# Two-block transformer kernel on one core: attention steps of block 2 in a new order, band copies on ScalarE's queue, memory projections in block 1

## What is computed

```python
z = jnp.einsum('bsd,df->bsf', x, w_in[l])
q_na, k_na, v_na, q_g, k_g, v_g, q_m, gate_logits = jnp.split(z, _split_points(), axis=-1)
y_na = ...   # neighbourhood attention, 8 heads of 64, keys of a 32-column band on an 8 x 64 grid
y_gqa = ...  # grouped-query attention, 8 query heads, 2 key heads of 64, norm and rotary first
mkv = jnp.einsum('bmd,df->bmf', mem, w_mem_kv[l])
mk, mv = jnp.split(mkv, 2, axis=-1)
y_mem = ...  # 4 heads of 128 over the 256 memory tokens
branches = jnp.stack([y_na, y_gqa, y_mem], axis=2)
proj = jnp.einsum('bsgk,gkd->bsgd', branches, w_branch[l])
gates = jax.nn.sigmoid(gate_logits + b_gate[l]).reshape(B, S, N_BRANCH, D)
merged = jnp.sum(gates * proj, axis=2)
mix = jnp.einsum('bsd,de->bse', merged, w_out[l])
x = layer_norm(DN_ALPHA * x + mix, ln1_g[l], ln1_b[l])
ffn = expert_choice_ffn(x, w_router[l], w_gate_up[l], w_down[l])   # 16 experts, 64 tokens each
x = layer_norm(DN_ALPHA * x + ffn, ln2_g[l], ln2_b[l])
```

## Time and profile before

| | us |
|---|---|
| median of 3 runs | 1814.62 |
| lowest, highest | 1810.46, 1818.32 |
| the profiled execution's own time | 1814.75 |
| its span, first to last instruction | 1812.8 |

### The profile page before, as it was taken

The page is one execution under the profiler, slowest core; times in us unless marked ns, Lnnn a source line. Parts: engine busy times, 40 slices in busy tenths (PEclk is TensorE's granted clock), DMA queues, the critical chain, the costliest instruction groups (busy, mean ns, idle before and its releaser), DMA issues.

```text
span 1812.8 us, 20763 instructions
## 1 busy us (share of the span) xinstructions
PE 1603.3 (88%) x7998; PEld 1136.4 (63%) x7998; DVE 745.2 (41%) x1091; ACT 516.2 (28%) x805; POOL 93.0 (5%) x144
## 2 busy tenths in 40 slices
PE   5989798999999989985799999998499999999994
PEld 4677677878878868864577787877333434434332
DVE  4454655334334344844434434355523222322235
ACT  4353424222221222243334433232021112111211
POOL 2000000000000001310111111000200000000000
PEclk9999579999999999987899999998599999999997
DMA  5222012323323335123112113337099999999993
GB/s 190 68 70 70 1 43 74 94 93 93 93 93 93 95 103 151 46 82 112 52 37 69 46 60 97 124 116 309 1 351 416 415 413 415 409 421 416 416 418 127
DMA packets 146038, 307.89 MB, mean 170 GB/s; under 512 B 8288, under 2 KB 99808, under 8 KB 129568
## 3 DMA queue, kind: packets, MB, share of 16 engines
q1 hardware_dynamic: 142592, 296.84, 44.5%
q0 software_dynamic: 2928, 9.02, 1.4%
q10 hardware_dynamic: 432, 0.81, 0.1%
HBM read 300.35 MB, written 4.56 MB: 168 GB/s over the span
## 4 chain that ended last, share of the span: by engine, by line
PE 73%; DMA 9%; DVE 8%; ACT 4%; issue 4%; SPq 1%; ACTq 0%; DVEq 0%
PE bank L948 11%; PE bank L1574 10%; PE bank L1575 9%; PE bank L1576 9%; DMA RING<-w_gu 5%; PE bank L1582 4%; PE bank L1583 4%; PE bank L1584 4%; DMA RING<-w_down 3%; PE bank L1621 2%; PE bank L923 2%; PE bank L1591 2%; PE bank L1592 2%; PE bank L1593 2%; PE bank L1709 2%
## 5 line engine op out<-in xcount | busy, mean ns | idle before, releaser
L1574 PE MATMUL bank<-XH,WH 128*128 128x512 f32 x768 | 305.6, 398 | 13.3 <-DVE WL L1278 12.2
L1575 PE MATMUL bank<-XL,WH 128*128 128x512 f32 x768 | 302.1, 393 | 0.0
L1576 PE MATMUL bank<-XH,WL 128*128 128x512 f32 x768 | 301.8, 393 | 0.0
L1278 DVE TENSOR_TENSOR WL<-RAW,WH 128x2048 fp32r<-128x2048 f32 (+1 forms) x91 | 194.2, 2134 | 178.9 <-ACT WH L1106 178.9
L948 PE MATMUL bank<-RING,XS 128*64 128x512 f32 x488 | 221.1, 600 | 16.9 <-DMA RING<-w_gu 9.0
L949 PE MATMUL bank<-RING,XS 128*64 128x512 f32 x496 | 224.7, 600 | 0.0
L1106 ACT ACTIVATE WH<-RAW 128x2048 fp32r<-128x2048 f32 (+1 forms) x91 | 161.8, 1778 | 170.8 <-PE bank L1584 124.8
L1574 PEld LDWEIGHTS bank<-XH,WH 128*128 128x128 f32 x768 | 146.6, 191 | 46.6 <-DVE WL L1278 13.5
L1576 PEld LDWEIGHTS bank<-XH,WL 128*128 128x128 f32 x768 | 146.0, 190 | 30.9
L1575 PEld LDWEIGHTS bank<-XL,WH 128*128 128x128 f32 x768 | 146.3, 190 | 30.3 <-issue 0.2
L948 PEld LDWEIGHTS bank<-RING,XS 128*64 128x64 f32 x488 | 63.4, 137 | 147.4 <-issue 142.6
(11 more groups left out here) (280 smaller groups left out, 2497.1 us busy)
## 6 DMA issues: line engine op xcount, KB each, us to landing
RING<-w_gu SPq DMA_DIRECT2D x123, 1024.0 KB, 13.7
RING<-w_down SPq DMA_DIRECT2D x64, 1024.0 KB, 11.7
RAW<-w_in SPq DMA_DIRECT2D x66, 512.0 KB, 4.8
RAW<-w_ffn_in SPq DMA_DIRECT2D x44, 512.0 KB, 4.6
RAW<-w_ffn_out SPq DMA_DIRECT2D x20, 512.0 KB, 4.3
RAW<-w_out SPq DMA_DIRECT2D x16, 512.0 KB, 4.7
RAW<-w_branch SPq DMA_DIRECT2D x24, 256.0 KB, 3.1
ONCE<-w_gu SPq DMA_DIRECT2D x5, 1024.0 KB, 11.1
```

The source lines that it names most:

```text
L1278: V.tensor_tensor(WL[:, u % 2, :n], RAW[:, u % 2, :n], WH[:, u % 2, :n].bitcast(F32), ALU.subtract).then_inc(s["w_lo"], 1)
L1574: T.matmul(bank[:, :st.nt], wh[:, k, c], hi, start=k == 0, stop=False)
L1575: T.matmul(bank[:, :st.nt], wh[:, k, c], lo, start=False, stop=False)
L1576: ins = T.matmul(bank[:, :st.nt], wl[:, k, c], hi, start=False, stop=k == st.K - 1)
```

## The change

**The lag.** In the three attentions of block 2, T, C and O of an iteration stand two iterations later instead of one, N one iteration later instead of none, and T and C stand ahead of X of the current iteration:

```diff
         turn = (((s_step, 0), (w_step, 0), (t_step, 1), (c_step, 1), (o_step, 2), (fill_step, 0)) if kind == "stick" else
-                ((s_step, 0), (x_step, 0), (t_step, 1), (c_step, 1), (n_step, 0), (fill_step, 0), (o_step, 1)))
+                ((s_step, 0), (t_step, 2), (c_step, 2), (x_step, 0), (n_step, 1), (fill_step, 0), (o_step, 2)))
```

```diff
     def na_band():
-        bands.append(add("band", dict(band=16 * 16), half=len(bands)))
+        bands.append(add("band", {f"band{len(bands) // 4}": 16 * 4}, half=len(bands) // 4, h=len(bands) % 4))
...
+            elif k == "band":
+                wait(act, "evA", st.at)
+                wait(act, "evD", st.at)
+                cols = slice(256 * st.half, 256 * st.half + 256)
+                bs = (0, 8, 24, 32)[st.h]
+                for b in range(2):
+                    for a in range(2):
+
+                        act.dma_start(VB[(2 * b + a) * 32:(2 * b + a) * 32 + 32, st.h, :, cols],
+                                      VN[a * 64 + bs:a * 64 + bs + 32, b::2, cols]).then_inc(s[f"band{st.half}"], 16)
```

```diff
-            9: [lambda: add("lsplit", dict(yhi=4, ylo=4), after=qkv[1])], 12: [lambda: out_half(0, 0)]}
+            9: [lambda: add("lsplit", dict(yhi=4, ylo=4), after=qkv[1])], 10: [memk(0)], 12: [memk(1)],
+            14: [lambda: out_half(0, 0)]}
...
     rms(X, XN, D, after=plan[-1])
+    memv(0)()
     tx(XN, XH, XL, KT, TT, scale=V_GFFN, feeds="x")
...
     fin = rms(X, X, D, grow=GFIN, after=plan[-1])

+    mem_last = memv(1)()
     save = add("save", dict(saved=16))
```

```diff
-    small = pieces_of(nak(1), nav(1), memk(0), memk(1)) + [memv(0), memv(1)] + pieces_of(gate(0, 0))
-    slots = (0, 1, 2, 3, 4, 5, 6, 7, 8, 10, 12, 14)
+    small = pieces_of(nav(1), nak(1), *(gate(0, j) for j in range(4)))
+    slots = (0, 1, 2, 3, 5, 6, 8, 9, 11, 12, 14, 15)
     fill = {i: [f] for i, f in zip(slots, small)}
-    fill[3].append(na_band)
-    na_last = attention("na", 4, 4, fill, lambda i: bands[i // 8])
+    for i in range(1, 5):
+        fill.setdefault(i, []).append(na_band)
+    na_last = attention("na", 4, 4, fill, lambda i: bands[4 * (i // 8) + 3])
...
-    small = pieces_of(gqm(1), branch(0, 0), *(f(0, j) for j in range(1, 4) for f in (gate, branch)))
+    small = pieces_of(gqm(1), *(branch(0, j) for j in range(4)), gate(1, 0), gate(1, 1))
...
-    small = pieces_of(*(f(1, j) for j in range(4) for f in (gate, branch)))
+    small = pieces_of(branch(1, 0), branch(1, 1), gate(1, 2), branch(1, 2), gate(1, 3), branch(1, 3), gate(2, 0),
+                      gate(2, 1))
...
-    add("reload", {})
-    for j in range(4):
-        whole(gate(2, j))
-        whole(branch(2, j))
+    for f, j in ((branch, 0), (branch, 1), (gate, 2), (branch, 2), (gate, 3), (branch, 3)):
+        whole(f(2, j))
+        if f is branch and j == 0:
+            add("reload", {})
```

More of the change, by code:

```diff
@@ L142, in build @@
     QM = at("QM", R0 + 32, [P, 4, S])
-    RT = at("RT", 181.5, [P, 3, 640])
+    RT = at("RT", R0 + 48, [P, 3, 640])
     GFIN = at("GFIN", R0 + 16, [P, D])
     LNR = at("LNR", 64, [P, 2, D])
-    GT = at("GT", 76, [P, 2, S])
+    GT = at("GT", 72, [P, 2, 2, S])
     MG = at("MG", R0 + 48, [P, KT, S])
@@ L203, in build @@
                lexp lgl lt lm2 lsq lin lrec ysq yn yhi ylo qk mx e_ab msk p tr ptA ptD pv o rope rxn rope_p
-               ms_hi ms_lo saved band x2h x2l xal lgp lgs afp af top ixp icc rcp pn ohi""".split()
+               ms_hi ms_lo saved band0 band1 x2h x2l xal lgp lgs afp af top ixp icc rcp pn ohi""".split()
     names.extend(["rms_q", "rsd_q"])
@@ L347, in build, with memk, memv @@
     win, win2 = w_in[0], w_in2[0]
+    def memk(j):
+        return lambda: unit(w_memkv[0], UC * j, KT, "F", "copy", dst=lambda r: MKT[:, 2 * j + r, :], src="m", nt=M)
+    def memv(j):
+        return lambda: unit(w_memkv[0], 512 + UC * j, KT, "T", "copy", dst=lambda r: MV[:, :, UC * j:UC * j + UC],
+                            src="m", nt=M)
     rms(X, XN, D, ready=x_in)
@@ L418, in gqm, with gate_home @@
         return (win2, 2304 + UC * j, KT, "F", "scaled"), dict(dst=lambda r: QM[:, 2 * j + r, :], scale=float(P) ** -0.5)
-    def memk(j):
-        return (w_memkv[0], UC * j, KT, "F", "copy"), dict(dst=lambda r: MKT[:, 2 * j + r, :], src="m", nt=M,
-                                                           over_rope=True)
-    def memv(j):
-        return lambda: unit(w_memkv[0], 512 + UC * j, KT, "T", "copy", dst=lambda r: MV[:, :, UC * j:UC * j + UC],
-                            src="m", nt=M, over_rope=True)
+    def gate_home(g, j):
+        return MG[:, 2 * j:2 * j + 2, :] if g == 0 else GT[:, j % 2, :, :]
     def gate(g, j):
@@ L460, in build @@
     rope_tile(3)
+    na_band()
     whole(naq(1))
-    small = pieces_of(nak(1), nav(1), memk(0), memk(1)) + [memv(0), memv(1)] + pieces_of(gate(0, 0))
-    slots = (0, 1, 2, 3, 4, 5, 6, 7, 8, 10, 12, 14)
+    na_band()
+    na_band()
+    small = pieces_of(nav(1), nak(1), *(gate(0, j) for j in range(4)))
+    slots = (0, 1, 2, 3, 5, 6, 8, 9, 11, 12, 14, 15)
     fill = {i: [f] for i, f in zip(slots, small)}
-    fill[3].append(na_band)
-    na_last = attention("na", 4, 4, fill, lambda i: bands[i // 8])
+    for i in range(1, 5):
+        fill.setdefault(i, []).append(na_band)
+    na_last = attention("na", 4, 4, fill, lambda i: bands[4 * (i // 8) + 3])
     tx(GQT, QG, None, 4, TT, f32=True, const=0.125, loose=True)
@@ L993, in _ @@
             sp.dma_start(X[:, t, :], xv[t]).then_inc(x_in[t], 16)
-        landed_v = []
         for st in plan:
-            if st.kind == "band":
-                landed_v.append(st)
             if st.kind == "unit":
@@ L1011, in _ @@
                         sp.dma_start(dst[:, kk, :], src[:, kk, :]).then_inc(raw_in[u % 2], 16)
-                while landed_v:
-                    v = landed_v.pop()
-                    wait(sp, "evA", v.at)
-                    wait(sp, "evD", v.at)
-                    cols = slice(256 * v.half, 256 * v.half + 256)
-                    for cb, bs in enumerate((0, 8, 24, 32)):
-                        for b in range(2):
-                            for a in range(2):
-                                sp.dma_start(VB[(2 * b + a) * 32:(2 * b + a) * 32 + 32, cb, :, cols],
-                                             VN[a * 64 + bs:a * 64 + bs + 32, b::2, cols]).then_inc(s["band"], 16)
                 if u == 1:
@@ L1108, in evacuate @@
         def evacuate(st, now):
-            if "over_rope" in st.kw:
+            if st.evac == "gate" and st.kw["g"] == 0:
                 wait(act, "rope", now.at)
                 wait(act, "rope_p", now.at)
-            if st.evac == "gate":
-                wait(act, "band", now.at)
+                wait(act, "res", mem_last.end)
             for r in now.now:
@@ L1127, in evacuate @@
                     wait(act, "evD", now.at)
-                    ins = A(GT[:, r, :], bank[:, :], ACT.Tanh, scale=0.5,
+                    ins = A(gate_home(st.kw["g"], st.kw["j"])[:, r, :], bank[:, :], ACT.Tanh, scale=0.5,
                             bias=vec(V_BG + 8 * st.kw["g"] + 2 * st.kw["j"] + r))
@@ L1281, in evacuate @@
         def evacuate(st, now):
-            if "over_rope" in st.kw:
-                wait(dve, "rope", now.at)
-                wait(dve, "rope_p", now.at)
             for r in now.now:
@@ L1311, in evacuate @@
                     dve.wait_ge(s["evA"], now.at["evA"])
-                    m, g = MG[:, 2 * st.kw["j"] + r, :], GT[:, r, :]
+                    m, g = MG[:, 2 * st.kw["j"] + r, :], gate_home(st.kw["g"], st.kw["j"])[:, r, :]
                     if st.kw["g"] == 0:
@@ L1694, in _ @@
                 wait(pe, "evD", st.after.end)
-                wait(pe, "band", st.after.end)
                 wait(pe, "tx_hi", st.after.end)
@@ L1712, in _ @@
                 a = st.a
+                for name in ("band0", "band1"):
+                    wait(pe, name, a.after.end)
                 wait(pe, "ptA", a.c.end)
```

## The result

The changed kernel takes 1774.08 us (median of 4 runs, 1773.22 to 1778.17), the kernel before 1815.40 beside it: a ratio of 0.9766, with 95% confidence 0.974 to 0.9791. The forecast was 1768, with a range of 1752 to 1790. The profiled execution took 1774.22 us; its span is 1772.4, 40.4 shorter than before.

A forecast was written before the change was run, and what follows sets the result against it. TensorE, busy for 88% of the span, was taken as the bound. Terms of -27.4, -10.8, +1.4, -21.6 and +12.0 sum to -46.4, taking the span from 1812.8 to 1766.4 and the execution to 1768 us, range 1752 to 1790.

The forecast's parts named there:

- NA: Block 2's NA stretch: 95.0 us of work plus idle pieces and 5 us of clock loss, 110.8 after, gain 27.0.
- What bounds the kernel: Whole kernel: TensorE, busy 88% of the span, so gains come only from its idle time and low-clock stretches.
- They have two causes. The first three come from SP's queue.: NA's idle times: 1.86, 7.72 and 16.04 us come from weights issued behind 16 band copies on SP.
- ScalarE's issue price: Band copies on ScalarE: 0.6 us to issue each, 2.4 a group, 19.2 in all.
- Covered: NA: a fill piece of 5.4 us covers a band group's issue on ScalarE; iteration 3's uncovered group costs 2.35 us.
- Block 1's attention: Two `memk` units there, 11.4 us of work, cost 8, bounds 5 and 13; faster clock returns some 3 to 6.
- Final norm: `memv(1)` at block 1's final norm costs 3.0 us, from the 2.29 split and transposes waiting for freed banks.
- GQA: GQA stretch: one gate unit less (10.8 us), 3.9 of stalls gone, 4 back; gain 10.8.
- The experts behind it are not touched.: Experts at the kernel's end: claimed unaffected, with no term in the sum.
- Rival 3: Block 1: the memory units cost their full work, 22.8 us instead of 12.0; time 1779, chance 0.10.
- Rivals 2 and 5: Rival 2: bands cost DMA time, 1794, chance 0.06. Rival 5: TensorE stays at 1.2 GHz through NA, 1848, chance 0.05.
- Rival 4: More gain: no NA clock loss (-5), third group hidden (-2.4), block 1 stretch (-3), smaller tail; 1756, chance 0.12.

The follow-up runs named there:

- the lag alone: Kernel before with only block 2's attention steps reordered (transposes, copy and output two iterations behind, scaling one): 1805.88 us, ratio 0.994.
- twice the copies: Changed kernel with each of its 32 band copies cut in two, the same bytes: 1791.96 us, ratio 0.9859.
- the one with the gates behind: Changed kernel with the two gate units it moved into the memory attention put back behind it: 1770.76 us, ratio 0.9765.
- the one with other fills: Changed kernel with NA's twelve fill pieces in other iterations, leaving 5, 8, 11 and 14 without a fill: 1784.25 us, ratio 0.9824.

## Why the prediction was right, and where its steps were off

The size and the mechanism held: NA gave 26.2 of 27.0 us, by the idle times that the prediction named, and the time is 6 us above the forecast. Some luck is in that: five terms came out worse than forecast by 11.2 us together, and five better by 5.3, of which 2.6 (the stretch with `gqm(0)` and the rest) were not in the sum at all.

- *What bounds the kernel.* Right: TensorE's busy time changed by 4 us, its idle time in NA by 28.6.
- *NA.* Work and clock, taken as 95 and 5, are 100.45 busy. The idle pieces were 0.7 and 1.05 in the forecast, 0.73 to 0.84 and 0.78 in the rows, and 3.09 behind iteration 3. The loss of some 2.4 was forecast and its place was not: the prediction lets the transposes slip by 2.35, through the scaling on GpSimd, and gives that iteration 4.1 of idle time. In the rows the wait stands ahead of the output, released by the copy PT, and the transposes behind it wait only 0.26, 3.35 in all. Moving the groups away from there took 2.36.
- *"They have two causes. The first three come from SP's queue."* The cause is right. The cure isn't the other queue alone: in groups of four SP's queue delays no weights within NA either; what it costs is 3.4 us ahead of it. And the lag alone took 3.4 of the 16.04.
- *ScalarE's issue price.* 0.6 forecast, 0.64 measured. "Covered" was right at this price only; at twice the copies two of the covers in NA fail.
- *Block 1's attention.* +10.6 against 8, within the bounds of 5 and 13 (whose middle is 9, not 8). How far this term is off can't be told from one pair of traces. From its first scores to the first product on its output the same code took 148.5 to 155.2 us in ten kernels that differ from the changed one only behind it or not at all, and 144.5 and 146.8 in the kernel before and the one with the lag alone. The rows are the kernel before, the changed one, and the one with the gates behind:

```profile
129.05:273.50 144.45, 127.12 (x616) 102.71 (x617) 79.92 (x151) 55.37 (x111) 0.00 (x0) 0.79 0.14 44
129.28:284.13 154.85, 136.67 (x712) 112.85 (x713) 85.18 (x155) 59.86 (x115) 0.00 (x0) 0.82 0.17 55
128.07:276.55 148.48, 129.18 (x713) 106.50 (x713) 85.11 (x155) 59.70 (x115) 0.00 (x0) 0.89 0.18 57
```

  The last two do the same work and idle about as long (18.2 and 19.3 us); they differ by the clock, 0.82 and 0.89. So "a long product brings the clock back, and what follows runs faster" gave 1.9 us in one trace (9.5 more busy for 11.4 of work) and 9.3 in another. VectorE is busy for 80 to 85 us of the stretch: it sets the pace in the 20 us from 206, and not throughout.
- *Final norm.* 3.0 as forecast, with the split and the wait for banks where they were expected.
- *GQA.* Off by 2.0. The idle pieces sum to 5.1, not 4 (and the prediction's own terms to 10.7, not 10.8), and TensorE's busy time fell by 9.95 (116.11 to 106.16) where a gate of 10.8 left.
- *"The experts behind it are not touched."* True of the code, but the router stage ahead of them took 4.9 us more. This is the largest single miss:

```profile
1254.10:1272.40 18.30, 14.33 (x97) 13.84 (x98) 10.26 (x11) 9.88 (x14) 7.12 (x4) 0.69 0.67 281
```

This is the kernel before, with a mean clock of 0.69; the changed kernel runs the same 97 matmuls at 0.50. Both profiles of kernels built on the one before show 18.2 to 18.3, nine of those built on the changed one 23.2, and a tenth, the one with doubled copies, 20.1. In the kernel before the clock came back within the stage, for the 6.9 us of the next row, and in the changed one it didn't:

```profile
1258.00:1264.90 6.90, 6.90 (x65) 6.90 (x64) 3.48 (x3) 3.70 (x7) 0.00 (x0) 0.99 1.02 430
```

It is neither the wait ahead of the stage nor the order of gates. What decides it stays open.

Rival 3 (block 1 at full price) fits this pair of traces for the keys (10.6 of 11.4; the shortest trace of the same code gives 4.0), and not for the values (3.2 of 11.4); its reason, VectorE as the slow engine, holds for part of the stretch only. Rivals 2 and 5 didn't come: no weight lands late in NA, and its clock is 0.97. Rival 4's items came in part (tail) and were eaten up elsewhere.

## What to carry to other kernels

Look for the copy that stands in an engine's queue behind work that it doesn't need, and let it lag one iteration more: that was worth 15 to 16 us in NA here. Put DMA issues on a computing engine only in groups that the next product covers, and check the iteration after each group, not the one that holds it. Filling TensorE's wait gains nothing where another engine is busy throughout: look at that engine's busy time in the stretch first. And before a term is called off by some us, look how far the same code lies apart in other traces: here by up to 6.7 us in one stretch.

## What the runs showed of the hardware

- The same wait costs more clock in one kernel than in another. Ahead of the output projection each kernel waits 3.60 us. Behind it the first matmul ran at either clock, and the clock fell in both (the changed kernel, then the one with other fills; each with the 10 us from that matmul on):

```profile
1158.50 0.47 PE L1584 MATMUL bank<-WH,XH 128*128 128x512 f32 x1 [3.60 <-DVE XL L1526]
1158.50:1168.50 10.00, 10.00 (x37) 8.09 (x38) 7.55 (x10) 4.57 (x7) 1.07 (x2) 0.83 0.40 152
```

```profile
1167.88 0.77 PE L1584 MATMUL bank<-WH,XH 128*128 128x512 f32 x1 [3.60 <-DVE XL L1526]
1167.88:1177.88 10.00, 9.99 (x32) 8.03 (x33) 7.65 (x10) 4.58 (x7) 1.07 (x2) 0.71 0.43 142
```

  That makes 51.3 or 52.4 us up to the router's transposes. From the last output to there it is 100.9 or 103.7 with the same code, as the clock also falls behind the last output in the second (0.89 in the 15 us from there, 1.00 in the changed kernel). With the 6.7 us between the shortest and the longest of block 1's attention, a forecast of one trace of this kernel can't be trusted to a few us.
- TensorE's clock was at half while it was busy for 9.38 of 9.50 us, with matmuls of 16 columns and eight transposes (the router stage above).
- GpSimd's 5.59 us beside VectorE lengthened VectorE's work by 4.25.
